# Three of the four modulations as fill steps of three sink-attention tiles

## The reference, cut to what matters

```python
def ada_norm(x, c, w, b, g):
    m = jax.nn.silu(c) @ w + b              # w: 1024 x 3072
    shift, scale, gate = jnp.split(m[:, None, :], 3, axis=-1)
    return rmsnorm(x, g) * (1 + scale) + shift, gate
```

## Time and profile before

| | us |
|---|---|
| median of 3 runs | 4101.93 (4093.4 to 4102.85) |
| the profiled execution | 4112.55 |
| its span, first to last instruction | 4111.0 |

### The profile page before, as it was taken

The page is one execution under the profiler, slowest core; times in us unless marked ns, Lnnn a source line. Parts: engine busy times, 40 slices in busy tenths (PEclk is TensorE's granted clock), DMA queues, the critical chain, the costliest instruction groups (busy, mean ns, idle before and its releaser), DMA issues. The chain is left out here.

```text
span 4111.0 us, 53886 instructions
## 1 busy us (share of the span) xinstructions
PE 3575.6 (87%) x20685; PEld 2102.0 (51%) x20917; DVE 2129.3 (52%) x3527; ACT 1365.0 (33%) x2660; POOL 479.5 (12%) x1002
## 2 busy tenths in 40 slices
PE   6867888777697999999978888888888899999996
PEld 3535455544353555555534555555554455555553
DVE  4644444445445555555545554555544655555553
ACT  5534444344323122222124444444432222122122
POOL 0002122223110000000000222211200000000000
PEclk9888887778798999999989999999998999999998
DMA  7721122112311111111121333333331011111111
GB/s 290 276 59 59 58 83 75 54 47 62 102 35 45 38 47 41 37 47 42 40 66 38 115 115 110 115 105 111 106 114 55 29 47 42 37 47 41 37 37 47
DMA packets 222722, 303.33 MB, mean 74 GB/s; under 512 B 24848, under 2 KB 174969, under 8 KB 221910
## 3 DMA queue, kind: packets, MB, share of 16 engines
q1 hardware_dynamic: 193046, 190.24, 13.9%
q0 software_dynamic: 29504, 110.77, 8.4%
HBM read 264.23 MB, written 63.95 MB: 80 GB/s over the span
## 5 line engine op out<-in xcount | busy, mean ns | idle before, releaser
L96 PE MATMUL psum<-h,ffn_high 128*128 128x512 f32 (+1 forms) x2112 | 1035.9, 531 | 48.2 <-DVE hl L474 48.2
L98 PE MATMUL psum<-hl,ffn_high 128*128 128x512 bf16 (+1 forms) x2028 | 616.6, 337 | 0.0
L100 PE MATMUL psum<-h,ffn_low 128*128 128x512 bf16 (+1 forms) x2066 | 578.9, 332 | 2.9
L96 PE MATMUL psum<-actr,ffn_high 128*128 128x512 f32 (+1 forms) x1056 | 517.2, 530 | 15.7 <-DVE actl L807 15.7
L96 PEld LDWEIGHTS psum<-h,ffn_high 128*128 128x128 f32 x2112 | 409.4, 194 | 135.3 <-issue 43.9
L98 PEld LDWEIGHTS psum<-hl,ffn_high 128*128 128x128 bf16 x2112 | 206.3, 98 | 431.7 <-issue 372.8
L86 PE MATMUL psum<-h,attC_high 128*128 128x384 f32 x744 | 367.5, 494 | 40.2 <-DVE hl L474 23.2
L86 PE MATMUL psum<-h,attAB_high 128*128 128x384 f32 x648 | 333.6, 515 | 39.0 <-DVE hl L474 23.4
L784 DVE TENSOR_SCALAR y<-u,cvT 128x1168 f32<-128x1168 f32 x88 | 78.2, 888 | 530.0 <-ACT u L735 530.0
L98 PE MATMUL psum<-actl,ffn_high 128*128 128x512 bf16 (+1 forms) x1012 | 308.0, 337 | 0.0
L100 PE MATMUL psum<-actr,ffn_low 128*128 128x512 bf16 (+1 forms) x1034 | 290.3, 332 | 1.5
(11 more groups left out here) (441 smaller groups left out, 7129.6 us busy)
## 6 DMA issues: line engine op xcount, KB each, us to landing
ada_raw<-in_ada_w SPq DMA_DIRECT2D x48, 1024.0 KB, 7.7
ffn_raw<-in_w_up SPq DMA_DIRECT2D x88, 512.0 KB, 3.6
ffn_raw<-in_w_down SPq DMA_DIRECT2D x44, 512.0 KB, 3.7
raw_C<-in_cache_c_k POOLq DMA_DIRECT2D x64, 256.0 KB, 3.4
raw_C<-in_cache_c_v POOLq DMA_DIRECT2D x64, 256.0 KB, 3.0
out_ck_s<-in_cache_c_k POOLq DMA_DIRECT2D x8, 1984.0 KB, 8.7
out_cv_s<-in_cache_c_v POOLq DMA_DIRECT2D x8, 1984.0 KB, 14.3
attC_raw<-in_w_in_odd SPq DMA_DIRECT2D x24, 512.0 KB, 4.7
```

What stands on the lines that cost most here:

```text
L96: return pe.matmul(out, w, x[:, lo:hi], start=first and start, stop=last and stop, skip_group_check=True)
L98: return pe.matmul(out, top(w), xl[:, lo:hi], start=first and start, stop=last and stop, skip_group_check=True)
L100: return pe.matmul(out, wl, top(x[:, lo:hi]), start=first and start, stop=last and stop, skip_group_check=True)
```

## The change

Modulation 0 stays in the setup. Modulations 1 to 3 are cut into 18 units `(a, j, half)` of 512 columns and put behind the `F` steps of tiles 4 (7 units), 5 (4 units) and 6 (7 units). A unit is four `D` steps, each with a chunk of its own of 512 KB (two slices of 128 rows, in pieces of 2 KB), four matmuls of 512 columns each, and one `M` step, which stands behind the unit after its own: four small matmuls turn the 18 rows, VectorE adds the bias and makes `gs`. ScalarE copies a unit's rows out after its fourth `D`. A `W` step stands before each next `D`. The biases come in as one load in the setup and are turned there. SP gets 72 loads more in these tiles and 36 fewer in the setup, GpSimd three fewer. The bank and the wait of every `F`, `P`, `D` and `M` step are now worked out ahead by `place()`, which goes through the steps and takes the two banks in turn; the matmuls of the setup write 18 rows instead of 128. All tiles get the late slots (`late = 1`). `osb`, `rtmp` and `W` lie or are sized otherwise to make room. The restore waits for the last `F` chunk of tile 6.

```diff
@@ -193,7 +193,9 @@
 
-FBASE = 4 * 3 * (KT // 2)
+FBASE = 3 * (KT // 2)
+ADA = [(a, j, h) for a in range(1, 4) for j in range(3) for h in range(2)]
+ADA_OF_TILE = {4: ADA[0:7], 5: ADA[7:11], 6: ADA[11:18]}
 
@@ -240,6 +242,7 @@
         sp.dma_start(vrow[40:41, :], ins["subln_g"]).then_inc(S.vec_in, 16)
+        sp.dma_start(brow[:, :], ada_b.rearrange("a (n p) -> (a n) p", p=P)).then_inc(S.vec_in, 16)
         for l in range(2):
@@ -254,7 +257,7 @@
         sp.dma_start(xrow[:, QB, :], ins["x_sample"].rearrange("b t d -> (b t) d")).then_inc(S.x_in[QB // 2], 16)
-        for a in range(4):
+        for a in range(1):
             for j in range(3):
@@ -348,8 +349,8 @@
                         cols = slice(D * (k % 2) + 512 * h, D * (k % 2) + 512 * (h + 1))
-                        pe.matmul(ps[:, 2 * (u % 2) + h, :], cst[:, k, :], w[:, cols], start=(k == 0), stop=False)
-                        mm = pe.matmul(ps[:, 2 * (u % 2) + h, :], cb[:, k, :], wl[:, cols],
+                        pe.matmul(ps[0:2 * NC9, 2 * (u % 2) + h, :], cst[:, k, :], w[:, cols], start=(k == 0), stop=False)
+                        mm = pe.matmul(ps[0:2 * NC9, 2 * (u % 2) + h, :], cb[:, k, :], wl[:, cols],
                                        start=False, stop=(k == KT - 1))
@@ -875,7 +877,7 @@
     lead, early = (0, 0) if last else (6, 4)
-    late = 0 if fill == "q" else 1
+    late = 1
     for u in range(QB + 1):
@@ -903,6 +905,10 @@
         [("F", name, b, k) for name in fill for b in range(3) for k in range(KT)]
+    ada = ADA_OF_TILE.get(T, [])
+    for d, unit in enumerate(ada):
+        todo += [("D",) + unit + (q,) for q in range(4)] + ([("M",) + ada[d - 1]] if d else [])
+    todo += [("M",) + ada[-1]] if ada else []
     seen = sent = 0
@@ -914,11 +920,14 @@
             turn, later = later, []
-        steps += todo[sent:upto]
         for f in todo[sent:upto]:
+            if f[0] == "D":
+                steps += turn
+                turn = []
+            steps.append(f)
             if unit_ends(f):
                 turn += [("W",)]
-                later += [("R", f[1])] if f[1] in ("q", "k") else []
+                later += [("R", f[1])] if f[0] == "F" and f[1] != "v" else []
         sent = upto
@@ -926,7 +935,7 @@
 
-    return s[0] == "F" and s[2:] == (2, KT - 1) or s[0] == "P" and s[2:] == (2, KT - 2)
+    return s[0] == "F" and s[2:] == (2, KT - 1) or s[0] == "P" and s[2:] == (2, KT - 2) or s[0] == "D"
 
@@ -946,7 +955,7 @@
         out.append((k, T, fill, c))
-        c += len(fill)
+        c += len(fill) + 4 * len(ADA_OF_TILE.get(T, []))
     return out, c + KT + 1
@@ -1071,6 +1079,37 @@
                 do_steps(do, kind, T, tile_steps(kind, T, fill, T == TL, nxt), cb + c)
+
+        def place():
+
+            turn, last, at = [1], {}, {}
+
+            def take(key, sem, value):
+                turn[0] ^= 1
+                at[key] = turn[0], last.get(turn[0])
+                last[turn[0]] = sem, value
+
+            def do(what, kind, T, s, c, turns):
+                if what == "F" and s[3] == 0:
+                    nk, nT = next_tile(kind, T)
+                    name, b = s[1:3]
+                    if T == T0 - 1 and name == "q":
+                        at[T, "F", name, b] = b, None
+                        last[b] = f_sem[name], f_no(name, nk, nT, b)
+                    else:
+                        take((T, "F", name, b), f_sem[name], f_no(name, nk, nT, b))
+                elif what == "P" and s[3] == 0:
+                    take((T, "P") + s[1:3], S.out_evac, 4 * KT * odd + 3 * s[1] + s[2] + 1)
+                elif what == "D" and s[4] == 0:
+                    take((T, "D") + s[1:4], S.ada_evac, 4 + ADA.index(s[1:4]))
+                elif what == "M":
+                    take((T, "M") + s[1:4], S.mod_evac, 2 + ADA.index(s[1:4]))
+                elif what == "VT":
+                    at[T, "VT"] = last[0], last[1]
+                    last[0] = last[1] = S.v_rows, kv(kind, T) + 1
+
+            run(None, do)
+            return at
 
@@ -1143,6 +1184,11 @@
                     spills(c)
+                elif what == "D":
+                    a_, j, half, x = s[1:]
+                    ring.load(sp, c, ada_w[a_, 2 * x:2 * x + 2, :, j * D + 512 * half:j * D + 512 * half + 512].rearrange(
+                        "k p n -> p k n"), 0, ("p (k n) -> p k n", dict(k=2)))
+                    spills(c)
                 elif what == "F" and s[2:] == (2, KT - 1):
@@ -1178,7 +1224,7 @@
 
-                ring.done(sp, cb + tiles[-1][3] - 1)
+                ring.done(sp, cb + tiles[6][3] + len(tiles[6][2]) - 1)
                 for t in range(7):
@@ -1404,19 +1453,40 @@
                     w, wl = ring.ready(pe, c) if b == k == 0 else (ring.w[c % 2][:, :], ring.wl[c % 2][:, :])
+                    bank, free = at[T, "P", j, b]
+                    if k == 0:
+                        pe.wait_ge(*free)
                     if i == k == 0:
-                        pe.wait_ge(S.v_rows, n + 1)
-                        pe.wait_ge(S.q_evac, 3 * (T + 1))
                         pe.wait_ge(S.restored, gone + 32 * 6)
-                    elif i >= 2 and k == 0:
-                        pe.wait_ge(S.out_evac, 4 * KT * odd + i - 1)
                     elif i == 0 and k == KT - 2:
...
                     lo, hi = THIRDS[b]
-                    mm = mm3(pe, ps[:, i % 2, 0:hi - lo], w[:, k * P:(k + 1) * P], wl[:, k * P:(k + 1) * P],
+                    mm = mm3(pe, ps[:, bank, 0:hi - lo], w[:, k * P:(k + 1) * P], wl[:, k * P:(k + 1) * P],
                              h[:, k, lo:hi], hl[:, k, lo:hi], k == 0, k == KT - 2)
...
                         mm.then_inc(*((S.t_used[c % 2], 1) if b == 2 else (S.out_ready, 1)))
+                elif what == "D":
+                    x = s[4]
+                    bank, free = at[(T, "D") + s[1:4]]
+                    w, wl = ring.ready(pe, c)
+                    if x == 0:
+                        pe.wait_ge(*free)
+                    out = ps[0:2 * NC9, bank, :]
+                    for i in range(2):
+                        cols = slice(512 * i, 512 * i + 512)
+                        pe.matmul(out, G.cst[:, 2 * x + i, :], w[:, cols], start=(x == i == 0), stop=False)
+                        mm = pe.matmul(out, G.cb[:, 2 * x + i, :], wl[:, cols], start=False, stop=(x == 3 and i == 1))
+                    mm.then_inc(S.t_used[c % 2], 1)
+                elif what == "M":
+                    d = ADA.index(s[1:4])
+                    bank, free = at[(T, "M") + s[1:4]]
+                    pe.wait_ge(*free)
+                    pe.wait_ge(S.ada_evac, 4 + d)
+                    for n_ in range(4):
+                        mm = pe.matmul(ps[:, bank, 10 * n_:10 * n_ + 10], modrow[d % 2][:, n_ * P:(n_ + 1) * P],
+                                       K[0:2 * NC9, C_ADA:C_ADA + 10], start=(n_ == 0), stop=(n_ == 3),
+                                       skip_group_check=True)
+                    mm.then_inc(S.mod_mm, 1)
                 elif what == "S":
@@ -1612,11 +1670,13 @@
             done = [2 * AB_TENSORS * odd]
-
-            def split(c, turns):
-
-                if c + 2 < cb + total or not isinstance(turns, int):
-                    ring.split_high(act, c + 2, turns)
+            turn = [cb + 2]
+
+            def split():
+
+                if turn[0] < cb + total:
+                    ring.split_high(act, turn[0])
+                turn[0] += 1
 
@@ -1784,19 +1850,37 @@
 
-            def split(c, turns):
-                if c + 2 < cb + total or not isinstance(turns, int):
-                    ring.split_low(dve, c + 2, turns)
+            turn = [cb + 2]
+
+            def split():
+                if turn[0] < cb + total:
+                    ring.split_low(dve, turn[0])
+                turn[0] += 1
 
...
                 if what == "W":
-                    split(c - 1, turns)
+                    split()
                 elif what == "R" and not odd:
...
                     out_third(s[1], s[2], c)
+                elif what == "M":
+                    a_, j, half = s[1:]
+                    d = ADA.index(s[1:4])
+                    dve.wait_ge(S.mod_mm, 2 + d)
+                    n0 = 8 * j + 4 * half
+                    y = ps[:, at[(T, "M") + s[1:4]][0], 0:40].rearrange("p (n c) -> p n c", n=4)[:, :, 0:NC9]
+                    i_ = dve.tensor_tensor(G.mod[:, a_, n0:n0 + 4, :], y,
+                                           G.bT[:, a_, n0:n0 + 4].unsqueeze(2).broadcast_to([P, 4, NC9]), ALU.add)
+                    if j == 1:
+                        ch.then(i_)
+                        g0 = 8 * a_ + 4 * half
+                        i_ = dve.scalar_tensor_tensor(
+                            out=G.gs[:, a_, 4 * half:4 * half + 4, :], in0=G.mod[:, a_, n0:n0 + 4, :], scalar=1.0,
+                            in1=G.gT[:, g0:g0 + 4].unsqueeze(2).broadcast_to([P, 4, NC9]), op0=ALU.add, op1=ALU.mult)
+                    i_.then_inc(S.mod_evac, 1)
```

(22 more changed lines are left out.)

40 lines of the change are left out of this document (20 added, 20 removed).

## The result

The changed kernel takes 4164.49 us (median; 4149.75 to 4169.16 over 4 runs) against 4099.04 for the kernel before in the same measurement: a ratio of 1.0155, interval 1.0124 to 1.0185. The change is slower by 65 us; the forecast was slower by 28. That lies inside the 8 in 10 range (4085 to 4175) and above the forecast's own (4110 to 4155). The profiled execution took 4169.16 us, its span is 4167.1.

What follows compares the result with a forecast made beforehand. The prediction took the setup as a chain of its own and the three tiles as paced by a round trip between engines per query block. 151 us added less 123.4 gave 28 slower, 4130 us; forecast's range 4110 to 4155, 8 in 10 4085 to 4175.

Steps and rivals of the forecast that it cites:

- setup: Before the first attention: the norm's first square comes at 86.3 us instead of 209.76, a gain of 123.4 us.
- D steps with ring and cover: In T = 4, 5 and 6: 144 us for 72 D steps, 11 for the ring, less 15 of cover.
- M steps: In T = 4, 5 and 6: 18 M steps at 0.6 us each, 11 us, bounds 0 and 45.
- rotation moved: In T = 4 and 6 the rotation of q comes earlier, in the blocks; its stall and 4.1 us only move.
- SP's tail: In the setup: SP's last chunk and three dependent writes end at 77.2 us, under 86.3 by 9 us.
- The ring rival: In T = 4 to 6 only the two-deep chunk ring sets the pace: 88 us added, 4067 us in all; chance 0.15.
- the clock rival: In T = 4 to 6 a higher granted clock gives part back, about the same time, 4102 us; chance 0.12.
- Everything additive at half clock: In T = 4 to 6: all costs add, no cover, 33 us for D steps before transposes; 210 us, 4189 total; chance 0.13.
- The 2.0 us a step: Each D step adds 2.0 us to a block's round trip, read from two places showing 2.05 and 2.07 us.
- The ring's 11 us: Where three or more D steps stand together, the two-deep raw buffers add 0.95 us to about 12 steps: 11 us.
- The 15 us of cover: In the stream parts of the three tiles, longer tiles hide waits for transfers: -15 us, bounds 0 and -30.
- The narrower output: In the modulation matmuls: 18 output rows instead of 128 change nothing, bounds -2 and +2 us.

Runs made afterwards that it cites:

- wide: The changed kernel with the modulation matmuls' stationary operand read 128 columns wide instead of 18; 4146.19 us, ratio 1.0103 to the kernel before.
- bare: lean_rlate with the 18 M steps left out as well, the later modulations set to constants; 4049.79 us, ratio 0.9877 to the kernel before.
- lean_rlate: the lean kernel with the rotation of q kept late, in the second stream half of T = 4 and 6; 4061.78 us, ratio 0.9895 to the kernel before.
- the lean kernel: The changed kernel with the loads, casts, subtractions and matmuls of D steps all cut to a few columns; 4067.71 us, ratio 0.9898 to the kernel before.
- r_late: wide with the rotation of q kept late, in the second stream half of T = 4 and 6; 4152.66 us, ratio 1.0121 to the kernel before.
- no_pe: The changed kernel with the D steps' matmuls cut from 512 to 8 columns; 4148.63 us, ratio 1.0115 to the kernel before.
- small_load: The changed kernel with each D load cut to 16 of 512 columns a slice; 4151.08 us, ratio 1.0119 to the kernel before.
- narrow: The kernel before with only the modulation matmuls' stationary operand cut from 128 to 18 columns; 4123.41 us, ratio 1.005.
- m3_spread: Only modulation 3 moved, 12 D steps each into T = 4 and 6, matmuls of 128 columns; 4129.26 us, ratio 1.0052 to the kernel before.

## Why the prediction was wrong where it was

The direction held: round trips between the engines, not the ring or the idle shares, set the price. The size did not, and neither did the account of what a D step's price is made of. The spans differ by 56.1 us and the medians by 65, against 28. By the terms of the sum, from one execution each:

| term | forecast | shown | by |
|---|---|---|---|
| setup | -123.4 | -119.8 | profile; -124.6 in wide |
| D steps with ring and cover | 144 + 11 - 15 = 140 | 148.4, of it 6.4 the narrow operand | what is left: 171.3 less the two rows below |
| M steps | 11 | 14.3 | bare less lean_rlate, in the lean kernel |
| rotation moved | 0 | 8.6 (3.3 in the full kernel) | lean_rlate, r_late |
| tiles, sum | 151 | 171.3 | profile |

**Right.** The price of the D steps stands as a sum: 148.4 less 6.4 is 142 us for 72 of them, 1.97 each, ring and cover in it. The block with four took 12.96 us. SP's tail never mattered. The rest from T = 7 on is shifted, not stretched. The ring rival fell, and so did the clock rival: the tiles took 128.7 to 140.9 us, and the clock went down in T = 5 and 6 and from 0.72 only to 0.74 in T = 4. The rival "Everything additive at half clock" had 210 us for the tiles and 4189 in all: the 171.3 lie nearer the forecast, the 4164 nearer this rival. Its 33 us for D steps ahead of transposes are not what no_pe shows (13 us for all the matmuls), nor are its 1.2 us for an M step. Its clock was partly there: in 768 to 779 us of T = 4 the granted clock is 0.50 and a pair takes 1.07 us, so a D step 2.1, over the prediction's upper bound of 1.86; in 786 to 789 us, at 1.00, it takes 1.30. The Trainium skill has the rule ("TensorE: Matmul & The Clock Gate", "HAM oscillation — how this bites in real kernels") that TensorE, when it waits for a transfer at every tile, falls back to the half clock each time. The 0.68 to 0.77 of the three tiles goes that way, though what TensorE waits for here is mostly VectorE's subtraction (22.0 us in T = 4).

**Luck in it.** The 2.0 us a step had two supports, "Two places, one answer". The block of T = 5 from 943.50 to 950.31 held more than a cast and a subtraction; ScalarE also copied out a third of a projection ahead of the cast of the probabilities:

```profile
945.51 0.48 ACT L1642 COPY f_q_AB<-psum 128x384 f32<-128x384 f32 x1
```

The block of 4.76 us has no such copy, and with it the probabilities' low part comes 0.5 us later after the maxima (3.01 us against 2.49). So some 0.5 of the 2.05 us is the copy's, and that place shows about 1.5; the other shows 2.07. The make-up was wrong too: taking nearly all of the cast and the subtraction away gave back 0.75 us a step (54 / 72), not 1.9, all three costs together 1.3 (94.5 / 72), and 0.75 us a step stayed in bare. The ring's 11 us compare with 8 in small_load. The 15 us of cover no run shows.

**The failed step** is "The narrower output (18 rows instead of 128) streams the same 512 columns; I give it nothing, bounds -2 and +2 us, since the matmuls there wait for VectorE's subtraction". The columns that are streamed were the same, but with 18 columns held two matmuls follow less closely than with 128: 0.65 against 0.46 us a pair. It costs 4.75 us in the setup, 6.4 in the tiles (both by wide, the second unsure), and 17.1 in a setup of 48 chunks (narrow). I had not carried it to the D steps at all. Without it the setup ends 1.1 us ahead of the forecast, and that near hit is in part luck: in wide ScalarE's last copy starts at 75.06 instead of 74.2, and the turning matmuls take 8.07 instead of 9.75 us.

**The second** is that the rotation's "stall and 4.1 us move, they don't go", priced at nothing. In a block, a D step's subtraction, TensorE's transposes and ScalarE's exponentials wait behind VectorE's rotation: the block with it took 14.66 us where 9 were forecast, and 7.98 without it (r_late). In T = 4 about half of that comes back behind the block; what is left over the tiles in the full kernel lies between 3.3 and 8.6 us. The division above follows the lean kernel, so 5 us may belong to the D steps instead.

**The third** is the M step: 0.8 us, not 0.6. Its matmuls are not the reason: in T = 4 of the changed kernel 56 records take 10.5 us, 0.19 each, against the 0.20 I took. Which of its waits makes the rest I did not separate.

**A fourth, also priced at nothing,** is "The projection steps of these tiles are packed tighter, at no cost". Before any D step, VectorE's first five pairs of maxima in T = 4 start within 22.9 us, against 20.4 in the kernel before; in T = 6 within 23.3 against 20.8. In m3_spread, with less to pack, it is 20.4 in T = 4. How much of these 2.5 us a tile comes back later in it was not measured.

These, with 2 us more for the D steps, make 3.6 + 20.3 = 24 of the 28 us between the two spans' difference and the forecast; the other 4.6 lie in T = 7 (-1.6) and behind it (+6.3), where no D step was added. The rest up to the medians' 65 is the choice of execution: the profiled one lies 13.5 us above the median of before in this measurement and 4.7 above that of after; the forecast took 10.6 for both.

**Is there a place where the move pays?** None of those tried. In the setup a D step's worth of work costs 1.73 us (124.6 / 72, by wide; 41.8 / 24 in m3_spread gives 1.74), where the transfers already take 0.80 of the DMA engines; in the sink-attention tiles 2.25 to 2.8, M steps in it, and in T = 7 3.4 to 3.8. With the narrow operand mended and the rotation put back, some 2.25 with its M step stay. A deeper ring in T = 7, where landings do end waits, was not tried.

## What to carry to other kernels

Work that needs three engines in turn is not hidden by the idle time of each: price it by what one such step adds to the round trip of the stage where it is put, and compare that with what it costs where it is. To find what such a step is made of, cut its parts one at a time and all together; here the single cuts gave 75 us, the joint one 94.5, and 76.8 stayed with almost no work left: the moved rotation, the M steps, the small matmuls and the hand-overs. When a price is read from one block against another, list all that differs between the two. When an edit makes an operand narrower, look at the interval between successive matmuls, not at the length of one.

## What had not been expected of the hardware

A stationary operand of 18 columns makes back-to-back matmuls of 512 moving columns slower than one of 128: 0.65 us against 0.46 a pair, both at a granted clock of 1.00, with shorter records (0.40 against 0.58 us for the first of the pair) and the weight loads no longer issued ahead. Matmuls of 8 moving columns with such an operand still took 0.18 to 0.22 us each on average in T = 4 of lean3, at a mean granted clock of 0.63.
